# Beginning two units of the output projection inside an attention stage, instead of one

## The reference

```python
# layer 0 ("fox"): 16 heads of 64, causal softmax with a decay added to the logits
h = concat_heads(softmax(q @ k.T * scale + c_q - c_k) @ v) @ w_out
x = layer_norm(ALPHA * x + h)
x = layer_norm(ALPHA * x + conv_ffn(x))
# layer 1 ("diff"): 8 heads, two softmaxes each, their weighted difference times v
a = softmax(q1 @ k1.T) - lam * softmax(q2 @ k2.T)
o = a @ v;  o = o * rsqrt(mean(o * o)) * gain      # per head and position
h = concat_heads(o) @ w_out
x = layer_norm(ALPHA * x + h)
```

## Time and profile before

| what | value |
|---|---|
| median of 3 runs | 2441.45 us (2439.8 to 2443.44) |
| the profiled execution, its own time | 2443.44 us |
| its span | 2441.6 us |
| granted TensorE clock, mean | 0.946 |
| PE busy | 2254.6 us, 92% |
| DVE, ACT, POOL busy | 1096.0, 1001.4, 974.8 us |
| tail of the fox layer, start of unit `ao` 0 to its last wait | 236.5 to 268.4 us |
| tail of the diff layer, start of unit `bo` 0 to its last wait | 920.2 to 970.9 us |
| chain that ended last | PE 84%, DVE 5%, ACT 4%, POOL 4%, issue 2% |

### The profile page before, as it was taken

One profiled execution on the slowest core, in us unless ns is written; L12 is line 12 of the kernel. 1 busy time (PEld: TensorE's weight loads), 2 busy tenths in 40 slices (PEclk: granted clock), 3 DMA queues, 4 the chain that ended last, 5 costly groups with the idle time before them and its releaser, 6 DMA issues.

```text
span 2441.6 us, 28073 instructions
## 1 busy us (share of the span) xinstructions
PE 2254.6 (92%) x10880; PEld 1841.6 (75%) x10880; DVE 1096.0 (45%) x1774; ACT 1001.4 (41%) x2015; POOL 974.8 (40%) x760
## 2 busy tenths in 40 slices
PE   7999999999979887999999789996899997999997
PEld 6778778888867776788888666664687885888886
DVE  3545555553345764555443333546545234232222
ACT  5665454443254553444442244443344234232222
POOL 3554644333455641644334351103423345232232
PEclk9999999999989998999999887997999997999998
DMA  4111222222212220222322111110012221222221
GB/s 152 51 65 58 70 87 91 100 101 95 97 61 75 77 83 18 70 101 90 104 97 95 59 46 35 35 35 18 18 44 95 86 104 52 104 87 104 97 95 50
DMA packets 29844, 183.07 MB, mean 75 GB/s; under 512 B 3984, under 2 KB 4112, under 8 KB 11920
## 3 DMA queue, kind: packets, MB, share of 16 engines
q1 hardware_dynamic: 29712, 181.27, 21.5%
HBM read 174.97 MB, written 2.10 MB: 73 GB/s over the span
## 4 chain that ended last, share of the span: by engine, by line
PE 84%; DVE 5%; ACT 4%; POOL 4%; issue 2%; DMA 1%; SPq 0%; POOLq 0%; ACTq 0%; DVEq 0%
PE PS L1239 82%; PE PS L1332 1%; POOL LO L2382 1%; POOL XL L2382 1%; PE PS L1442 1%; DVE bQS L1899 1%; DVE cCVT L2266 0%; DVE aQS L1899 0%; DMA RAW<-wall 0%; POOL A_p L2402 0%; POOL bROT L2430 0%; ACT bP L1739 0%; POOL A_c L2402 0%; PE PS L1380 0%; POOL bTQ L2435 0%
## 5 line engine op out<-in xcount | busy, mean ns | idle before, releaser
L2382 POOL TENSOR_TENSOR LO<-RAW,HI 128x512 fp32r<-128x512 f32 (+1 forms) x382 | 542.3, 1436 | 686.9 <-ACT HI L1530 686.9
L1239 PE MATMUL PS<-XH,HI 128*128 128x512 f32 (+1 forms) x1584 | 645.1, 407 | 40.7 <-POOL XL L2382 20.5
L1239 PE MATMUL PS<-XH,LO 128*128 128x512 f32 (+1 forms) x1584 | 628.1, 397 | 0.0
L1239 PE MATMUL PS<-XL,HI 128*128 128x512 f32 (+1 forms) x1584 | 628.1, 397 | 0.0
L1899 DVE TENSOR_TENSOR LO<-RAW,HI 128x512 fp32r<-128x512 f32 (+3 forms) x286 | 313.5, 1102 | 290.9 <-ACT HI L1530 290.7
L1530 ACT ACTIVATE HI<-RAW 128x512 fp32r<-128x512 f32 (+3 forms) x668 | 365.1, 608 | 170.6 <-PE PS L1239 167.2
L1239 PEld LDWEIGHTS PS<-XH,HI 128*128 128x128 f32 (+1 forms) x1584 | 303.7, 192 | 132.5 <-issue 57.3
L1239 PEld LDWEIGHTS PS<-XH,LO 128*128 128x128 f32 (+1 forms) x1584 | 302.9, 191 | 66.6 <-issue 1.1
L1239 PEld LDWEIGHTS PS<-XL,HI 128*128 128x128 f32 (+1 forms) x1584 | 304.2, 192 | 58.4 <-issue 1.0
L1239 PE MATMUL PS<-HH,HI 128*128 128x512 f32 x528 | 205.4, 389 | 0.0
L1239 PE MATMUL PS<-HL,HI 128*128 128x512 f32 x528 | 205.4, 389 | 0.0
(11 more groups left out here) (380 smaller groups left out, 3352.3 us busy)
## 6 DMA issues: line engine op xcount, KB each, us to landing
RAW<-wall SPq DMA_DIRECT2D x138, 1024.0 KB, 4.8
RAW<-wall SPq DMA_DIRECT2D x24, 896.0 KB, 4.4
bROT<-bTQ SPq DMA_DIRECT2D x64, 64.0 KB, 2.0
RAW<-wall SPq DMA_DIRECT2D x5, 512.0 KB, 3.2
XF<-xT SPq DMA_DIRECT2D x4, 512.0 KB, 6.0
outT<-XR SPq DMA_DIRECT2D x8, 256.0 KB, 2.0
FP<-cfp SPq DMA_DIRECT2D x1, 1024.0 KB, 6.8
MKF<-cmask SPq DMA_DIRECT2D x1, 704.0 KB, 11.4
```

Of the source, the lines that this page charges most:

```text
L1239: return e.matmul(out, a, b, start=start, stop=stop)
L2382: return e.tensor_tensor(out, x, h.bitcast(F32), ALU.subtract)
```

## The change

The tail of each attention stage begins units 0 and 1 of the output projection, in four banks, in place of unit 0 in two. Unit 1 is taken once all scores are in the list (`free`), since its banks 2 and 3 are score banks. The split of unit 2, which has to wait for the end of unit 0, is held back (`held`) until the last step of unit 0 is written. The rates of rounds per tick in the two tails go from 0.9 to 0.75 and 0.45. The residuals of all four tiles stand behind the tail, ahead of unit 2.

```diff
-RATES = (0.37, 0.18, 1.15, 0.36, 1.0, 0.9, 0.9)
+RATES = (0.37, 0.18, 1.15, 0.36, 1.0, 0.75, 0.45)
-    def lin_begun(key, src):
-        def reached(kk):
-            if (src, kk) not in ready:
-                until(lambda: (src, kk) in ready)
-        ts = lin_fm(key, src, together=True, before=reached)
-        drain()
-        lin["banks"] = [2, 3, 4, 7, 0, 1]
-        lin["n"] = 0
+    def lin_pair(keys, src, banks, made, free):
+        ts = []
+        def begin(q):
+            i = take(keys[q])
+            for j in range(2):
+                tiles.append(Tile([(i, k) for k in range(8)], 128 * j, 128, banks[2 * q + j], src))
+                ts.append(len(tiles) - 1)
+        def rows(some, *kks):
+            for kk in kks:
+                if not made(kk):
+                    until(lambda: made(kk))
+                for t in some:
+                    step_of("mm", t, kk)
+                    tick()
+        begin(0)
+        rows(ts, 0, 1, 2, 3)
+        if not free():
+            until(free)
+        begin(1)
+        held, due[0] = due[0], None
+        rows(ts[2:], 0, 1, 2, 3)
+        rows(ts, 4, 5)
+        rows(ts[:2], 6, 7)
+        due[0] = held
+        rows(ts[2:], 6, 7)
         return ts
...
         beside[1] = RATES[5]
-        return lin_begun(("ao", 0), "aO")
+        ts = lin_pair([("ao", 0), ("ao", 1)], "aO", [0, 1, 2, 3], lambda kk: ("aO", kk) in ready, lambda: sent[0] == 64)
+        drain()
+        lin["banks"] = [4, 7, 0, 1, 2, 3]
+        lin["n"] = 0
+        return ts
     def attn_out(name, src, n, begun=None):
-        for i in range(4):
-            for j, t in enumerate(lin_fm((name, i), src) if i else begun):
+        for j, t in enumerate(begun):
+            residual(n, j, t)
+        for i in (2, 3):
+            for j, t in enumerate(lin_fm((name, i), src)):
                 residual(n, 2 * i + j, t)
         layer_norm(n)
...
         beside[1] = RATES[6]
-        return lin_begun(("bo", 0), "bO")
+        ts = lin_pair([("bo", 0), ("bo", 1)], "bO", [0, 1, 2, 3], lambda kk: ("bO", kk) in ready, lambda: sent[0] == 32)
+        drain()
+        lin["banks"] = [4, 7, 0, 1, 2, 3]
+        lin["n"] = 0
+        return ts
```

## The result

| | before | after |
|---|---|---|
| median (8 runs each) | 2440.62 us (2431.22 to 2449.14) | 2459.47 us (2453.94 to 2470.61) |
| span of the profiled execution, clock | 2441.6 us, 0.946 | 2457.2 us, 0.947 |

The ratio is 1.0084, 95% interval 1.0056 to 1.0110. The medians lie 18.8 us apart, and the interval lies wholly above 1: slower, by 0.8%.

The account below looks back on a forecast made before the run. PE, busy 92% of the span, was taken as the bound, so only its idle time and clock count. Fox +10.2 and diff +7.6 gave +17.8 us on 2441.45: 2459 us, own range 2454 to 2467.

Parts of the forecast that it names:

- The stall: PE waits at unit 2's row block 2 for GpSimd's LO 1; 10.5 us a layer, ready 14.7 after E, unit 0's last matmul.
- The clock behind the stall: PE's matmuls after each stall start at the low clock; costs 1.5 us a stall, bounds 1.2 and 2.3.
- The fox tail: In the fox tail, waits for `aOL` and `aPX` go and small costs return; net -1.8 us, bounds -2.2 and -1.2.
- The diff tail: In the diff tail, -1.4 us of idle and -3 us from the clock; net -4.4 us, bounds -6.4 and -1.4.
- Nothing gives this back, GpSimd has caught up one unit later: After the stall, unit 3 and the layer norm follow with PE as the bound, so the loss stays.
- The first rival: The stall is covered and only the tails' terms are left, -6.2 us: 2435 us; chance 7%.
- The short stall: GpSimd's adds start earlier or PE arrives late at low clock; stall 7 us a site, 2451 us; chance 17%.

Follow-up runs that it names:

- `three_adds_out`: The changed kernel without GpSimd's adds of `YH` into A1 for tiles 1 to 3 of both attention layers; 2446.04 us, ratio 1.0018.
- `diff_alone`: The changed tail and rate in the diff layer only, the fox layer as in the kernel before; 2445.16 us, ratio 1.0027.
- `split_first`: The changed kernel with the rest of unit 2's split written ahead of the four residuals; 2445.91 us, ratio 1.0018.
- `sums_on_dve`: The changed kernel with unit 2's split ahead of the residuals, a reordered tail, and attention-layer sums of y on VectorE, not GpSimd; 2438.80 us, ratio 1.0005.
- `split_on_dve`: The changed kernel with unit 2's split ahead of the residuals and all LO pieces of units 2 and 3 on VectorE; 2457.55 us, ratio 1.0060.

## Why the prediction was right, and where its sizes were off

- **The stall** (10.5 us a layer): right in place, releaser and order. It measured 12.0 and 11.8, a little outside the upper bound of 11.7. I took two of six adds as slowed by VectorE; five of the six took 1.5 to 1.7 us, two adds of squares among them, which not even my upper bound had. LO 1 was ready at E + 15.9, not 14.7. The one add of 1.27 us ran almost wholly while VectorE was idle (284.94 to 287.33), the others beside its residuals or its LO pieces. The Trainium skill, "GPSIMD Engine Reference", section Specifications, that VectorE instructions with two SBUF inputs contend with GpSimd, was nearer than my count, and the trace agrees: VectorE's last `YH` of the four took 1.04 us in place of 0.69.

```profile
283.90 1.04 DVE L1962 SCALAR_TENSOR_TENSOR YH<-XH,YL 128x512 f32<-128x512 f32 x1
```

- **The clock behind the stall** (1.5): too small. Half clock lasted 5.3 us in fox and about 4.6 in diff, so it cost 2.6 and 2.3 us; my upper bound was 2.3. I had sized the term from the single stretch of 2.8 us in the earlier trace rows. The length does not follow the wait: behind the same 4.46 us at a layer norm half clock lasted 2.7 and 6.1 us in the two layers of `three_adds_out`, and behind the 10.6 us of `diff_alone` 3.6 us.
- **The fox tail** (-1.8): idle -1.7, right. The K wait is 2.7, and the new waits in `until` are 0.4 and 0.2.
- **The diff tail** (-1.4 idle, -3 clock): idle -1.9. The wait for a score bank came (1.92, I had 2.1), the tail's old `bP` wait went wholly, where I had left 0.9 of it, that for `bOT` grew from 0.7 to 2.1, which I had kept at 0.7, and `bOL` fell to 6.4, more than my 7.2. Busy time fell by 0.6 with 2.3 added by the stall, so the clock gave back 2.9: right.
- **What was not in the sum**: 1.2 us more of busy time in fox, and 2.2 us in the diff layer's statistics, which ran at half clock where before they had not (the `SQ_a` block 1.84 us, before 1.03). The second is not shown to come from the change, as said above.
- **"Nothing gives this back, GpSimd has caught up one unit later"**: true of the kernel after, where unit 3 and the layer norm have no new wait. But it says less than it seems to: GpSimd catches up because PE stands still for 12 us, and in `split_first`, where PE does not, unit 3 waits 3.7 us.
- **The first rival** (2435 if LO 1 stands ahead of the adds): its condition was met by `split_first` and its time did not follow. What failed in it is that -6.2 us is what remains once the stall is gone. Neither of the two orders tried took the waits away; they moved and cut them.
- **The short stall**: not seen; LO 1 was later than reckoned, and PE came at full clock in both layers.

By the stretches the terms should have summed to +25.8 and not +17.8 us, or to +23.6 without the diff statistics. The median, +18.8, lies close to the forecast partly by luck: in the two profiled executions the rest behind the diff layer was 10.9 us shorter after the change, which the change does not explain, the ratio's interval reaches from 13.7 to 26.8 us, and the lowest runs of the two kernels differ by 22.7.

## What to carry to other kernels

Before moving matmuls out of a stretch to fill a gap elsewhere, add up what every other engine still has to do in that stretch: here GpSimd had 27 us of work in 33.5, and taking 8 us from TensorE shortened it by 2 us at best. The sum is a first warning and not the answer: with 5 us less work on GpSimd the stretch stayed as long, because its adds also wait for VectorE and ScalarE. Look first at how much idle time the filled gap really loses (here 1.7 and 1.9 us out of 18), and set that against it. A wait that goes away when one piece is reordered has to be looked for further on, in the next unit and at the next reduction.

## What the runs showed of the hardware that was not expected

**The same work at two lengths.** Behind the diff layer all kernels do the same work, and idle time is nearly the same. Windows of PE over that rest, of before, after and `sums_on_dve`:

```profile
1018.35:2441.60 1423.25, 1323.33 (x6146) 0.94 0.21 72
```
```profile
1044.83:2457.20 1412.37, 1311.18 (x6146) 0.95 0.21 72
```
```profile
1024.69:2434.20 1409.51, 1305.32 (x6135) 0.95 0.20 72
```

Idle is 99.9, 101.2 and 104.2 us, so the difference is busy time, at a clock of 0.94 in place of 0.95. Over the fourteen profiles nine rests lie at 1407 to 1414, four at 1421 to 1424, one at 1433. The runs fall in the same way: the twelve of `split_on_dve` are four from 2443.0 to 2446.4 and eight from 2456.2 to 2460.5. What decides it was not tried. How many of 4 to 12 runs fall on either side moves a median and a ratio, which fits that ratios and stretches above differ by up to 11 us.

**The price of a two-input GpSimd operation** on 128x512 went from 1.27 us to between 1.70 and 1.77 while VectorE made residuals or LO pieces. VectorE paid as well: two LO pieces beside GpSimd's adds took 3.0 us, where one alone takes 0.69. A product with the ones vector, one column wide, which sums over 128 partitions, shows as two matmul records of 0.14 to 0.17 us each here, so 28 of them cost 7.7 to 9.6 us.
